# MLA output projection inside the attention loop, and a router that reads raw transposes of x

## What is computed

```python
for i in range(2):
    h = rmsnorm(x, norm_mix[i])
    y = dilated_attention(h, dsa_w_in, dsa_w_out) if i == 0 else \
        mla(h, mla_w_in, q_norm, w_qb, kv_norm, w_kvb, mla_w_out)
    x = x + y
    h = rmsnorm(x, norm_moe[i])
    x = x + hier_moe(h, ...)      # top group of 4, top 2 of its 8 experts
    gate = sigmoid(rmsnorm(x, norm_ple[i]) @ ple_w_gate[i])
    x = x + (p[i] @ ple_w[i]) * gate
return rmsnorm(x, norm_final)
```

## Time and profile before

| | us |
|---|---|
| three runs, median | 1400.25 |
| lowest, highest | 1399.12, 1400.6 |
| the profiled execution | 1395.45 |
| its span, first to last instruction | 1393.7 |
| busy: TensorE matmul, weight load | 1054.6, 814.1 |
| busy: VectorE, ScalarE, GpSimd | 459.3, 290.1, 7.8 |
| chain that ended last | DMA 50%, TensorE 41%, VectorE 5% |

### The profile page before, as it was taken

How to read it: one execution, slowest core, us unless ns; L and a number is a source line. 1 busy time by engine, 2 the same in 40 slices (tenths; PEclk the granted TensorE clock), 3 DMA queues, 4 the chain that set the end, 5 groups by cost and what they waited for, 6 DMA issues and landing times.

```text
span 1393.7 us, 30955 instructions
## 1 busy us (share of the span) xinstructions
PE 1054.6 (76%) x13756; PEld 814.1 (58%) x13756; DVE 459.3 (33%) x1021; ACT 290.1 (21%) x551; POOL 7.8 (1%) x17
## 2 busy tenths in 40 slices
PE   6999999977656666666667988987666666565667
PEld 6999999865534444454445645565454444444445
DVE  6545555542212111111114665431121211121127
ACT  5433444220100000000004444201000000000016
POOL 0000000000000000000000000000000000000000
PEclk9999999999889887988889999999888888889789
DMA  9986540689999999999999730489999999999991
GB/s 285 312 223 177 160 116 0 271 350 426 425 426 427 427 426 427 426 427 426 426 427 393 291 153 1 173 372 425 427 427 426 426 427 427 426 425 427 427 371 40
DMA packets 113483, 469.97 MB, mean 337 GB/s; under 512 B 4656, under 2 KB 78528, under 8 KB 88528
## 3 DMA queue, kind: packets, MB, share of 16 engines
q1 hardware_dynamic: 112672, 465.78, 83.5%
q0 software_dynamic: 688, 2.28, 0.5%
HBM read 466.99 MB, written 1.05 MB: 336 GB/s over the span
## 4 chain that ended last, share of the span: by engine, by line
DMA 50%; PE 41%; DVE 5%; issue 2%; ACT 2%; DVEq 0%; SPq 0%; ACTq 0%
DMA ring<-moe_w_down 28%; DMA ring<-moe_w_up 11%; DMA ring<-moe_w_gate 8%; PE ps L1549 6%; PE ps L1328 5%; PE ps L1330 5%; PE ps L1329 5%; PE ps L1564 4%; PE ps L1639 3%; DMA ring<-ple_w_gate 3%; PE ps L1442 2%; PE ps L1594 2%; PE ps L1392 1%; PE ps L1368 1%; PE ps L1463 1%
## 5 line engine op out<-in xcount | busy, mean ns | idle before, releaser
L1549 PE MATMUL ps<-ring,scr 128*32 128x128 f32 x8192 | 272.4, 290 | 136.4 <-DMA ring<-moe_w_up 85.4
L1549 PEld LDWEIGHTS ps<-ring,scr 128*32 128x32 f32 x8192 | 237.0, 116 | 175.9 <-DMA ring<-moe_w_up 97.5
L1564 PE MATMUL ps<-ring,scr 128*32 128x256 f32 x2048 | 176.2, 500 | 142.5 <-DMA ring<-moe_w_down 126.7
L1564 PEld LDWEIGHTS ps<-ring,scr 128*32 128x32 f32 x2048 | 84.0, 135 | 209.6 <-issue 143.9
L694 ACT COPY scr<-ps 32x256 f32<-32x256 f32 x128 | 46.6, 364 | 554.4 <-PE ps L1564 553.6
L1089 DVE TENSOR_TENSOR scr<-scr,ps 128x128 f32<-128x128 f32 x64 | 23.8, 371 | 405.9 <-PE ps L1549 405.9
L1102 DVE COPY scr<-ps 32x256 f32<-32x256 f32 x128 | 53.3, 417 | 272.5 <-PE ps L1564 271.7
L1328 PE MATMUL ps<-hT_hi,w_qk_hi 128*128 128x256 f32 x368 | 105.1, 286 | 0.0
L1330 PE MATMUL ps<-hT_hi,w_qk_lo 128*128 128x256 f32 x368 | 103.9, 282 | 0.0
L1329 PE MATMUL ps<-hT_lo,w_qk_hi 128*128 128x256 f32 x368 | 103.5, 281 | 0.0
L1594 PE MATMUL ps<-scr 128*128 128x512 f32 x128 | 71.2, 707 | 15.4 <-DVE scr L1102 15.4
(11 more groups left out here) (234 smaller groups left out, 1170.0 us busy)
## 6 DMA issues: line engine op xcount, KB each, us to landing
ring<-moe_w_gate SPq DMA_DIRECT2D x64, 2048.0 KB, 37.0
ring<-moe_w_up SPq DMA_DIRECT2D x64, 2048.0 KB, 35.8
ring<-moe_w_down SPq DMA_DIRECT2D x64, 2048.0 KB, 35.6
ring<-dsa_w_in SPq DMA_DIRECT2D x72, 512.0 KB, 6.5
ring<-ple_w_gate SPq DMA_DIRECT2D x4, 2048.0 KB, 36.4
ring<-dsa_w_out SPq DMA_DIRECT2D x2, 2048.0 KB, 13.7
ring<-mla_w_out SPq DMA_DIRECT2D x2, 2048.0 KB, 24.5
x_sb<-ple_w SPq DMA_DIRECT2D x2, 1024.0 KB, 10.5
```

The lines of the kernel that those rows point to most:

```text
L1549: mm = pe.matmul(bank(b)[CW * q:CW * q + CW, 0:P], xT[:, k, :], tile(t + j, KD, FF)[:, k, P * q:P * q + P], start=(k == 0), stop=(k == KD ...
L1564: mm = pe.matmul(bank(6)[CW * q:CW * q + CW, 0:T], e_hT[:, CW * j:CW * j + CW], tile(t + 2, FF // P, D)[:, j, T * q:T * q + T], start=(j = ...
```

## The change

1. The scores of all pairs go to banks 5 and 6. `m_scores(j)` on TensorE now waits until VectorE has added the mask of pair j-1 (`s_taken`).
2. Layer 1's projection of chunk 1 goes to banks 6 and 7 (`mix_bank`), that of chunk 0 stays in 0 and 1. `mix_early(c, k)` runs the products of one k for both halves n inside the attention loop: chunk 0's k = j-2 from step 2 on, chunk 1's k = 0 in step 6, and behind the loop chunk 0's k 5 and 6 and chunk 1's k 1 and 2 between turns and weighs.
3. ScalarE copies a pair's output ahead of the exponentials instead of behind.
4. In both layers the router reads raw transposes: `turn_x` transposes x itself once both halves are added; VectorE and ScalarE copy the turned rows out (`take_turned`, `norm_aside`). GpSimd multiplies the router by the gains `norm_moe` beforehand, and `choose` multiplies the logits by `rstd`. The host lays out router and gains accordingly. The norm's own chain (squares, root, scaling into `hs`) stays, for the gathers.
5. In `experts` on TensorE the order changes: the turns come right after a chunk's last add, `ranks(0)` stands ahead of the last product of chunk 1, the seeds go between the gathers, and `scattered` is signalled by the last seed behind the last gather.
6. The branch for experts with over 32 tokens gets its factors and gains in other places; the execution profiled here does not enter that branch. The experts' tiles of the main path keep their layout.

```diff
             for l in range(2):
                 if l == 1:
                     pool.wait_ge(S("logits_ready"), TC)
                 pool.dma_start(r_w, routers[l].rearrange("p (k n) -> p k n", k=KD)).then_inc(S("router_in"), 16)
+                pool.wait_ge(S("router_in"), 16 * (l + 1))
+                pool.wait_ge(S("wts_in"), 16)
+                pool.tensor_tensor(r_w, r_w, part(wts, W_ROUTER + KD * l, KD).unsqueeze(2).to_broadcast([P, KD, NR]),
+                                   ALU.mult).then_inc(S("router_ready"), 1)
...
+        def mix_bank(l, c, n):
+            return 6 + n if l == 1 and c == 1 else 2 * c + n
...
+            def norm_aside(l, c):
+                i = 3 * l + 1
+                square(i, c)
+                act.wait_ge(S("var_ready"), TC * i + c + 1)
+                act.activation(root[:, c:c + 1], root[:, c:c + 1], ACT.Sqrt, scale=1.0 / D).then_inc(S("root_ready"), 1)
+                act.wait_ge(S("hT_turned"), 4 * i + 2 * c + 2)
+                act.copy(hT[:, 4:8, c * P:(c + 1) * P], bank(5 + 2 * c, 4, P)).then_inc(S("xT_copied_a"), 1)
+                act.wait_ge(S("rstd_ready"), TC * i + c + 1)
+                scale(i, c)
...
             for j in range(MH // 2):
                 act.wait_ge(S("m_pT_ready"), j + 1)
                 act.copy(m_pT[j % 2][:, 1, :], bank(3)[:, 0:384]).then_inc(S("m_pT_copied_a"), 1)
+                if j >= 1:
+                    m_copy_o(j - 1)
                 if j + 2 < MH // 2:
                     m_exps(j + 2)
-                if j >= 1:
-                    m_copy_o(j - 1)
...
+            def take_turned(l, c):
+                dve.wait_ge(S("hT_turned"), 4 * (3 * l + 1) + 2 * c + 1)
+                dve.tensor_copy(hT[:, 0:4, c * P:(c + 1) * P], bank(4 + 2 * c, 4, P)).then_inc(S("xT_copied_d"), 1)
...
+            def variance(i, c):
+                square(i, c)
+                dve.wait_ge(S("sq_d"), TC * i + c + 1)
+                dve.wait_ge(S("sq_a"), TC * SCALED[i] + c + 1)
+                dve.scalar_tensor_tensor(out=root[:, c:c + 1], in0=ss[:, c:c + 1, 0], scalar=EPS * D,
+                                         in1=ss[:, c:c + 1, 1], op0=ALU.add, op1=ALU.add).then_inc(S("var_ready"), 1)
...
                 dve.wait_ge(S("logits_ready"), TC * l + c + 1)
                 lg, bias = bank(4)[:, c * NR:(c + 1) * NR], r_b[:, l * NR:(l + 1) * NR]
-                dve.tensor_tensor(r_lg[:, c, :], lg, bias, ALU.add)
-                link(dve.tensor_tensor(gp8[:, c, 0:NG], lg[:, 0:NG], bias[:, 0:NG], ALU.add))
+                root_of = rstd[:, c:c + 1]
+                dve.scalar_tensor_tensor(out=r_lg[:, c, :], in0=lg, scalar=root_of, in1=bias, op0=ALU.mult, op1=ALU.add)
+                link(dve.scalar_tensor_tensor(out=gp8[:, c, 0:NG], in0=lg[:, 0:NG], scalar=root_of, in1=bias[:, 0:NG],
+                                              op0=ALU.mult, op1=ALU.add))
...
             def experts(l):
-                norm_staged(3 * l + 1, add_mixed(l), lambda: choose(l, 0), lambda: place(l, 0))
+                i, add = 3 * l + 1, add_mixed(l)
+                add(0, 0)
+                add(0, 1)
+                variance(i, 0)
+                unroot(i, 0, 1)
+                scale(i, 0)
+                take_turned(l, 0)
+                add(1, 0)
+                choose(l, 0)
+                add(1, 1)
+                variance(i, 1)
+                take_turned(l, 1)
+                unroot(i, 1, 2)
+                scale(i, 1)
+                place(l, 0)
...
                 dve.wait_ge(S("m_s_ready"), j + 1)
-                src = ps[:, 0:2, 0:384] if j % 2 == 0 else ps[:, 5:7, 0:384]
-                link(dve.tensor_tensor(m_s[j % 3], src, causal, ALU.add))
+                dve.tensor_tensor(m_s[j % 3], ps[:, 5:7, 0:384], causal, ALU.add).then_inc(S("s_taken"), 1)
+                dve.wait_ge(S("s_taken"), HEADS + j + 1)
...
+            def turn_x(i, c):
+                for b in range(2):
+                    for k in range(4):
+                        mm = pe.transpose(bank(4 + 2 * c + b)[:, k * P:(k + 1) * P],
+                                          x_sb[:, c, (4 * b + k) * P:(4 * b + k + 1) * P], ident)
                     mm.then_inc(S("hT_turned"), 1)
...
-                        mm = pe.matmul(bank(2 * c + n), m_o[:, k, rows], tile(Tiles.MLA_OUT + n, KD, 512)[:, k, :],
...
                 def logits(c):
-                    pe.wait_ge(S("hT_ready"), 4 * SCALED[i] + 2 * c + 2)
-                    pe.wait_ge(S("router_in"), 16 * (l + 1))
+                    pe.wait_ge(S("xT_copied_d"), TC * l + c + 1)
+                    pe.wait_ge(S("xT_copied_a"), TC * l + c + 1)
+                    pe.wait_ge(S("router_ready"), l + 1)
                     for k in range(KD):
                         mm = pe.matmul(bank(4)[:, c * NR:(c + 1) * NR], hT[:, k, c * P:(c + 1) * P], r_w[:, k, :],
                                        start=(k == 0), stop=(k == KD - 1))
...
                     pe.wait_ge(S("choice_ready"), TC * l + c + 1)
                     count(bank(5)[:, NE * c:NE * c + NE], [(all_ones, d) for d in range(c)] + [(low, c)]).then_inc(S("ranks_ready"), 1)
-                def seed(c):
-
+                def seed(c, n):
+                    return pe.matmul(bank(2 * c + n), ident, x_sb[:, c, 512 * n:512 * n + 512], start=True, stop=True)
+                def turn_added(c):
                     pe.wait_ge(S("x_added"), 8 * l + 2 * c + 2)
-                    for n in range(2):
-                        mm = pe.matmul(bank(2 * c + n), ident, x_sb[:, c, 512 * n:512 * n + 512], start=True, stop=True)
-                    return mm
+                    turn_x(i, c)
+                def scaled(c):
+                    pe.wait_ge(S("hs_d"), TC * SCALED[i] + c + 1)
+                    pe.wait_ge(S("hs_a"), TC * SCALED[i] + c + 1)
                 for n in range(2):
                     mix_part(l, 0, n, [KD - 1])
-                turn_at, logits_at = (2, 6) if l == 0 else (0, KD // 2)
-                mix_part(l, 1, 0, range(KD) if l else range(BESIDE, KD))
-                mix_part(l, 1, 1, range(turn_at), last=False)
-                turn_rows(i, 0)
-                mix_part(l, 1, 1, range(turn_at, logits_at), last=False)
+                mix_part(l, 1, 0, range(BESIDE, KD))
+                turn_added(0)
+                if l == 0:
+                    mix_part(l, 1, 1, range(BESIDE), last=False)
                 logits(0)
-                mix_part(l, 1, 1, range(logits_at, KD))
+                mix_part(l, 1, 1, range(BESIDE, KD - 1), last=False)
                 ranks(0)
-                seed(0)
-                turn_rows(i, 1)
-                seed(1).then_inc(S("scattered"), 1)
+                mix_part(l, 1, 1, [KD - 1])
+                turn_added(1)
                 logits(1)
+                seed(0, 0)
+                seed(0, 1)
                 pe.wait_ge(S("oneh_first"), TC * l + 1)
+                scaled(0)
                 gather_first(0, 0)
                 ranks(1)
-
                 gather_first(0, 1)
+                seed(1, 0)
                 pe.wait_ge(S("oneh_first"), TC * (l + 1))
+                scaled(1)
                 for half in range(2):
                     gather_first(1, half).then_inc(S("gathered"), 1)
+                seed(1, 1).then_inc(S("scattered"), 1)
                 pe.wait_ge(S("xT_ready"), 2 * (NGRP + 1) * l + 1)
...
             pe.wait_ge(S("q_rot"), TC)
             def m_scores(j):
+                if j >= 1:
+                    pe.wait_ge(S("s_taken"), HEADS + j)
                 for h2 in range(2):
                     q, k = m_qT[0:QK, 2 * j + h2, :], m_kT[0:QK, 2 * j + h2, :]
-                    b = (5 if j % 2 else 0) + h2
+                    b = 5 + h2
                     pe.matmul(bank(b)[:, 0:P], q[:, 0:P], k[:, 0:P], start=True, stop=True)
                     mm = pe.matmul(bank(b)[:, P:3 * P], q[:, P:T], k, start=True, stop=True)
...
+            def mix_early(c, k):
+                if c == 0:
+                    pe.wait_ge(S("m_o_copied"), k + 1)
+                for n in range(2):
+                    mix_part(1, c, n, [k], last=False)
+            for n in range(2):
+                wait_tile(pe, Tiles.MLA_OUT + n)
             for j in range(MH // 2 - 1):
                 if j + 2 < MH // 2:
-
-                    pe.wait_ge(S("m_nmx"), j + 1)
                     m_scores(j + 2)
+                if j >= 2:
+                    mix_early(0, j - 2)
+                if j == MH // 2 - 2:
+                    pe.wait_ge(S("s_taken"), HEADS + MH // 2)
+                    mix_early(1, 0)
                 m_turn(j)
                 if j >= 1:
                     m_weigh(j - 1)
-
             m_turn(MH // 2 - 1)
+            mix_early(0, MH // 2 - 3)
             m_weigh(MH // 2 - 2)
+            for k in range(1, BESIDE):
+                mix_early(1, k)
             m_weigh(MH // 2 - 1)
-            for n in range(2):
-                wait_tile(pe, Tiles.MLA_OUT + n)
```

(7 more changed lines are left out.)

61 lines of the change are left out of this document (28 added, 33 removed).

## The result

| | median us | lowest to highest | executions |
|---|---|---|---|
| before | 1399.69 | 1395.79 to 1400.6 | 5 |
| after | 1388.83 | 1384.74 to 1391.07 | 5 |

The ratio is 0.9921, 95% interval [0.9908, 0.9934]: faster by 10.9 us, where 7.5 were forecast. Measured a second time the kernel after gave 1388.01 [0.9913, 0.9943]. The profiled executions tell another story: 1395.45 before and 1391.07 after, only 4.4 apart. Both facts have to be explained.

A forecast was written before the change was run, and what follows sets the result against it. Transfers at 426 to 427 GB/s bound the kernel, so only time ahead of each layer's plateau can be won: 5.2 (layer 1) + 2.3 (layer 0) = 7.5 us, giving 1392.7 against median 1400.25; range 1389.6 to 1396.6.

The forecast's parts named there:

- Layer 0: Before layer 0's plateau: 3.0 us of lacking traffic won, less 0.7 delay of three tiles: -2.3, bounds -3.0 and 0.
- Rival (b): Layer 0 gives nothing because the issue of its three tiles is held longer than reckoned: 1395.0, chance 0.10.
- The choice beside the iota: Layer 0's router: with GpSimd's iota moved behind it, the choice takes 2.7 us as in layer 1, instead of 3.19.
- Routing of layer 1: Last projection half to first expert: 14.2 us instead of 16.7, a gain of 2.5, bounds 1.0 and 3.8.
- rival (c): TensorE stays at 1.2 GHz through the routing, so logits, seeds and gathers lose 3 to 4: 1395.5, chance 0.08.
- ple_w: Its 1 MB transfer in layer 1 moves into the plateau's opening; 0.3 us remains in the way, bounds 0 and 2.5.
- The loop: Layer 1's attention loop: TensorE becomes the bound, steps 4.90 against VectorE's 3.70; last projection half ends 3.0 us earlier.
- Idle time won: TensorE's idle time in layer 1's attention loop, filled by projection products: 6.0 less 1.4 plus 0.6, so 5.2 us.
- The median: Gain of 7.5 taken from the 1395.45 execution, 4.8 under the median: 1387.9 for a like execution, 1392.7 against 1400.25.
- (a): Waits between engines in the loop's new order leave idle time standing; loop gains 0 to 1.5: 1395.0, chance 0.12.
- (d): One bank pair makes scores and VectorE take turns in the loop; steps of 8.6, six add 22: 1415, chance 0.04.
- (e): More than reckoned: gather at 2.3, no delay in layer 0, ple_w hidden: 1390.3, chance 0.11.

The follow-up runs named there:

- experiments 3: Idle, never-read matmuls (fillers) in TensorE's routing waits: three places in the kernel before, 1397.3 us (0.9984); four in the kernel after, 1388.25 us (0.9916).
- experiment 4: Kernel before with idle matmuls in three routing places and two more in the attention loop: 1395.11 us, ratio 0.9968.
- experiments 3 and 7: 7: kernel after with idle matmuls in routing and the loop's first steps, layer 0's last product ahead of the ranks: 1386.02 us, ratio 0.9898.
- the second execution: Profiled execution from timing both kernels again without edit: 1385.38 us after, 1400.36 before; medians 1388.01 after and 1400.36 before.
- the router alone: Router half of the change in both layers, attention loop and its projection as in the kernel before: 1393.36 us, ratio 0.9959.
- experiment 5: Kernel after with ranks(0) moved behind the projection's last product in both layers: 1387.63 us, ratio 0.9912 to the kernel before.
- the loop alone: Loop half of the change (bank pair, products in the loop, ScalarE's copy order), router as in the kernel before: 1395.01 us, ratio 0.9968.
- experiment 6: Kernel after with ScalarE's exponentials ahead of the output copy, as in the kernel before: 1391.95 us, ratio 0.9947 to the kernel before.

## Why the prediction was right or wrong

**Bounds: right.** The plateaus stayed at 426 to 427 GB/s, and the gain lies in the two stretches ahead of them.

**Layer 0: mechanism right, too large for a like execution.** Forecast -2.3. Its experts take 509.98, 510.45, 510.08, 510.42, 510.03, 510.41 and 507.96 with the new router, and 511.11, 513.99, 512.13 with the old one and no fillers: means 509.9 and 512.4, so -2.5. But against the execution that I took the sum from (511.11) it is -1.2, and against the old router with fillers (510.60 and 510.74 in experiments 3 and 4) -0.8. The windows give the same as the first of these: 300 to 310 lacks (427-397)/427 x 10 = 0.7 us of traffic after, instead of 3.0, so 2.3 are won, and the three tiles come 0.98 later instead of 0.7: -1.3. The gate's issue came 45.6 to 49.5 after the first tile's instead of 51.8. That 49.5 gave the same length as 46.8 fits the cover by transfers in flight that I argued with; but 45.6 gave 507.96 once and 510.41 once, so this stage scatters by more than what is asked of it. Rival (b), nothing won here, is nearer to a like execution than I allowed. The choice beside the iota was right as well. Timeline of VectorE and GpSimd after, layer 0, answering to the earlier trace rows:

```profile
279.29 0.26 DVE L1019 SCALAR_TENSOR_TENSOR scr<-ps,small,scr 128x36 f32<-128x36 f32 x1 [3.41 <-PE ps L1538]
...
281.47 0.17 DVE L1033 CAST small<-small_u 128x2 f32<-128x2 uint32 x1
...
282.09 0.19 DVE L1037 TENSOR_TENSOR scr<-scr 128x32 f32<-128x32 f32 x1
```

```profile
283.62 1.09 POOL L534 IOTA scr<- 128x1152 f32 x1 [254.83 <-PE ps L1381]
...
296.35 0.67 POOL L530 TENSOR_TENSOR scr<-scr,wts 128x288 f32<-128x288 f32 x1 [6.37 <-DMA scr<-routers]
```

With the iota behind it the choice takes 2.80 instead of 3.19 and its cast 0.17 instead of 0.45. The rule of the Trainium skill that the prediction gives (SBUF — State Buffer, a shared port locked whole) agrees with that. GpSimd's multiply took 0.67, between my bounds of 0.3 and 1.1, and nothing waited for it.

**Routing of layer 1: the sum right by luck, its parts off both ways.** Forecast 14.2, measured 14.14 and 14.13. But 13.1 is what the chain takes at full clock (experiments 3 and 7). The walk was 1.1 too long: the gather took 2.05 where I took 2.6, and it came 0.5 earlier than I walked, and 1.0 was lost to the lower clock, which I had given to rival (c) alone. Rival (c) therefore holds in its mechanism and fails in its size: 1.0 on the path, and another 1.7 in one of the two executions, not 3 to 4. Behind the second chunk's waits the granted clock was 0.75 (888.5 to 893.5) and 0.66 (885 to 890 in the second execution), not the 0.5 I had named as a sign. No run here separates the transposes from the waits beside them. ple_w was priced at 0.3 and no cost shows.

**The loop: mechanism right, terms mis-sized.** TensorE became the bound, and in the middle steps nothing waited. From the first query projection to the last half added it is 91.25 before and 88.20 in the profiled execution after, so -3.1 for my -3.0; but that contains 1.7 lost to the lower clock, eight matmuls at 5.38 instead of 3.68. In the second execution it is 86.51, as in both filled ones (86.50, 86.49), so -4.7. Of this, 0.6 lies ahead of the loop's first turn: the kernel before ran its first scores (2.40 instead of 1.41) and this turn at the lower clock even in the profile I took the sum from. Timeline and window of the kernel before:

```profile
831.71 1.48 PE L1766 MATMUL ps<-cst,hs 128*128 128x128 f32 x6
...
835.89 0.85 PE L1766 MATMUL ps<-cst,hs 128*128 128x128 f32 x6 [1.40 <-DVE scr L1301]
```

```profile
828.00:833.00 5.00, 3.69 (x15) 3.25 (x16) 3.28 (x10) 2.91 (x13) 0.00 (x0) 0.66 0.01 2
```

From the first turn on it is 4.1 for 3.0. Counted between starts of rows, my terms come out like this:

- Idle time won, 5.2: it is 6.0. I took the scores as the length of their rows to the idle gap (1.58), with the tail of the last matmul in it; where work follows at once they take 1.42. So each of the four middle steps had 0.70 to win and not 0.54, and the three waits behind them had such tails too. The step measured 4.69 instead of 4.90 for the same reason.
- The wait of the first pairs' scores, 0.4: it is there (0.39) and costs nothing, since the wait for VectorE behind it is there in both kernels (1.40 and 1.35); the first two turns are 4.18 apart before and 4.15 after.
- ScalarE's copy in step 6, 0.55: 0.54. The copies ahead of the first logits, 0.9: 0.89. Both right.
- Changes between kinds of matmul, 0.3: with the ranks ahead of the last product some 0.5, which is what the sum leaves over.

**The median: the step that failed.** "So 1387.9 for a like execution, and 1392.7 against the median 1400.25" carried the 4.8 between a short execution and the median over as if they were a constant around the kernel. They are not: the stages that the change touches are longer in other executions of the kernel before than in the one that I read. Without fillers the profiles give, in us (94.12 is the router alone, which has the old loop; 89.32 is experiment 5, which has the new one; layer 0's new values are those listed above, two of them with fillers; left out are the loop alone, whose last add comes late, and the other copy order of experiment 6; read is the profile that the forecast was made from):

| stage | read | old | mean | new | mean | gain, forecast |
|---|---|---|---|---|---|---|
| first query projection to last half added | 91.25 | 91.25, 92.66, 94.12 | 92.7 | 88.20, 86.51, 89.32 | 88.0 | 4.7, 3.0 |
| last add to first expert | 16.70 | 16.70, 17.49 | 17.1 | 14.14, 14.13, 14.13, 14.13 | 14.1 | 3.0, 2.5 |
| layer 0's experts | 511.11 | 511.11, 513.99, 512.13 | 512.4 | as above | 509.9 | 2.5, 2.3 |

Together 10.2, of the 10.9 and 11.2 by the medians. In the profile that I read, the kernel before stands 1.4, 0.4 and 1.3 under its means, 3.1 in all, and the gain exceeds the forecast by 3.4. These are few profiles, which scatter by 1 to 3 us in a stage, so the match is no better than that.

For a like execution the forecast of 7.5 is not far off, by compensation. Between 1395.45 and 1385.38 the touched stages differ by 8.0 (7.3 in attention and routing, 0.7 in layer 0), between 1395.45 and 1391.07 by 6.7 (5.6 and 1.1). The other 2.1 of the first pair's 10.1 lie in stages that the change does not touch: there 1385.38 is luck.

What lengthens the stages is in good part TensorE at the lower clock behind its waits. For the routing and layer 0 the fillers show it: 15.75 instead of 17.1, 510.7 instead of 512.4, and a median 2.2 lower (interval 0.7 to 3.6) in a kernel whose computation is the same. For the loop it is not shown. The profiles go with it: the longer executions have the clock down in it more often, as here in 835 to 840 of the second execution of before and in 831 to 836 of the router alone. But experiment 4's fillers did not lift it at the loop's start, and its 93.08 is no shorter.

```profile
835.00:840.00 5.00, 3.41 (x21) 2.78 (x22) 4.89 (x15) 3.63 (x16) 0.00 (x0) 0.68 0.00 0
```

```profile
831.00:836.00 5.00, 3.36 (x20) 2.60 (x21) 4.86 (x14) 2.87 (x11) 0.00 (x0) 0.80 0.00 0
```

The change takes such waits away (six of the loop's seven ahead of turns, the 2.00 of the routing, though it adds 0.72, 0.78 and 0.72 there). With fillers in both kernels the gain is 9.1 both times, not 10.9 or 11.2, so about 2 us of it is lost time that fillers remove as well, if the medians are good to that. And 9.0 and 9.2 of it lie in attention and routing by the profiles (108.63 to 99.61, 108.82 to 99.60).

**Rivals.** (a) appears only with the copy order of experiment 6. (c), by its own price of 3 to 4, would have been 1395.7 to 1396.7, not 1395.5. (d) never: steps of 4.69, not 8.6. (e), "more than reckoned", is what happened in kind. Its floor of 1390.3 was still too high, since it kept the 4.8; its three items make 1.3, so by them it should have stood at 1391.4.

**Open:** why the transfers of layer 1's experts took 1.7 us longer in the two filled kernels after (experiments 3 and 7) than in the others; what lengthens the loop of the kernel before; and how much of the scatter left in the kernel after is the untouched stage at 750 to 760, which no run filled.

## What to carry to other kernels

A forecast made from one profile should be compared with like executions, and the distance to the median is itself a term: look for windows under full clock behind waits, and ask which of them the change removes. A step's length should be taken between starts of rows that follow without a gap, since a row that ends in an idle stretch includes a tail that other work would cover. The stage lengths of several profiles of the same kernel, set side by side, tell more than one profile's total. Where engines pass work in a ring, the order of a copy and other work on a helper engine (3.9 us here, of the medians) can decide whether moved work is free.

## What the runs showed of the hardware

- Behind waits of 0.78 and 0.72 us around eight transposes the granted clock was down in both executions after (0.75 in 888.5 to 893.5, 0.66 in 885 to 890): the four seeds behind took 3.30 and 3.36 us, and 1.96 with two fillers of 0.6 us. The Trainium skill, TensorE: Matmul & The Clock Gate, section "HAM oscillation — how this bites in real kernels", tells of waits for transfers of some 3 to 5 us between short bursts that leave the engine throttled; these rows agree in kind, at waits of under 1 us each.
- The same kernel's stretches at 1.2 GHz fall in different places from execution to execution (285 to 295 in one profile after, none there in the next), and cost 1.7 us at one place.
- In the profile a GpSimd multiply of 128x288 took 0.67 us; a GpSimd iota of 128x1152, 1.09 us.
- A conversion of 128x2 values on VectorE took 0.45 us beside GpSimd's iota and 0.17 us without it.
